# The RWKV-7 recurrence of a two-block kernel: preparation and inversion of each round in one stage

## What is computed

```
S = S * w + (S @ -kk) (kk * a)^T + v k^T
y = S @ r
```

## Time and profile before

| | us |
|---|---|
| median of 3 runs | 2764.68 |
| lowest and highest run | 2762.72, 2766.3 |
| the profiled execution | 2762.08 |
| its span | 2759.1 |
| TensorE, VectorE, ScalarE busy in the span | 2668.9, 1884.4, 1205.4 |

### The profile page before, as it was taken

The page is one execution under the profiler, slowest core; times in us unless marked ns, Lnnn a source line. Parts: engine busy times, 40 slices in busy tenths (PEclk is TensorE's granted clock), DMA queues, the critical chain, the costliest instruction groups (busy, mean ns, idle before and its releaser), DMA issues. The chain is left out here.

```text
span 2759.1 us, 48978 instructions
## 1 busy us (share of the span) xinstructions
PE 2668.9 (97%) x19134; PEld 2281.0 (83%) x19134; DVE 1884.4 (68%) x3427; ACT 1205.4 (44%) x2294; POOL 285.1 (10%) x217
## 2 busy tenths in 40 slices
PE   7988899999999999999999999999999999999998
PEld 5868766778888789998878999989999857899997
DVE  3454668552332588887457888888888767788885
ACT  3232235531212454445256544465444438654444
POOL 2000114422111300001401000010000100100000
PEclk9999889999999999999999999999999999999999
DMA  8250310123232223334303333332333331323331
GB/s 279 63 169 16 111 38 5 62 77 107 92 95 88 77 77 97 110 92 124 92 17 92 89 104 96 104 107 86 109 99 101 83 86 26 92 79 113 92 108 54
DMA packets 369540, 248.89 MB, mean 90 GB/s; under 512 B 28692, under 2 KB 364376, under 8 KB 369312
## 3 DMA queue, kind: packets, MB, share of 16 engines
q1 hardware_dynamic: 368818, 245.18, 30.2%
q10 hardware_dynamic: 494, 0.59, 0.1%
HBM read 241.52 MB, written 2.12 MB: 88 GB/s over the span
## 5 line engine op out<-in xcount | busy, mean ns | idle before, releaser
L3018 ACT CAST dense_wt_hi<-ring 128x512 fp32r<-128x512 f32 x719 | 444.4, 621 | 462.5 <-PE bank L3068 220.5
L3023 DVE TENSOR_TENSOR dense_wt_lo<-ring,dense_wt_hi 128x512 fp32r<-128x512 f32 x719 | 493.6, 689 | 105.8 <-ACT dense_wt_hi L3018 104.4
L3055 PE MATMUL bank<-dense_operand_hi,dense_wt_hi 128*128 128x256 f32 x1248 | 353.7, 283 | 4.2 <-DVE h L3672 4.2
L3057 PE MATMUL bank<-dense_operand_hi,dense_wt_lo 128*128 128x256 f32 x1248 | 353.1, 283 | 0.0
L3056 PE MATMUL bank<-dense_operand_lo,dense_wt_hi 128*128 128x256 f32 x1248 | 353.1, 283 | 0.0
L3068 PE MATMUL bank<-dense_act_hi,dense_wt_hi 128*128 128x512 f32 x832 | 258.4, 392 | 0.8 <-DVE dense_act_lo L3336 0.8
L3068 PE MATMUL bank<-dense_act_lo,dense_wt_hi 128*128 128x512 f32 x832 | 257.1, 390 | 0.0
L3068 PE MATMUL bank<-dense_act_hi,dense_wt_lo 128*128 128x512 f32 x832 | 256.7, 390 | 0.0
L3055 PE MATMUL bank<-feat_hi,dense_wt_hi 128*128 128x256 f32 (+1 forms) x820 | 246.8, 301 | 7.5 <-DVE h L3707 3.2
L3055 PEld LDWEIGHTS bank<-dense_operand_hi,dense_wt_hi 128*128 128x128 f32 x1248 | 238.8, 191 | 12.2 <-issue 5.0
L3057 PE MATMUL bank<-feat_hi,dense_wt_lo 128*128 128x256 f32 (+1 forms) x820 | 245.8, 300 | 0.0
(11 more groups left out here) (726 smaller groups left out, 5429.3 us busy)
## 6 DMA issues: line engine op xcount, KB each, us to landing
ring<-in_ffn_w_up SPq DMA_DIRECT2D x88, 512.0 KB, 3.9
ring<-in_ffn_w_gate SPq DMA_DIRECT2D x88, 512.0 KB, 5.2
ring<-in_ffn_w_down SPq DMA_DIRECT2D x60, 512.0 KB, 4.8
ring<-in_ada_w SPq DMA_DIRECT2D x24, 1024.0 KB, 8.0
ring<-in_ffn_w_down SPq DMA_DIRECT2D x52, 256.0 KB, 3.9
ring<-in_w_ffn_gate SPq DMA_DIRECT2D x11, 1024.0 KB, 5.3
ring<-in_w_ffn_up SPq DMA_DIRECT2D x11, 1024.0 KB, 5.4
ring<-in_w_in SPq DMA_DIRECT2D x8, 1024.0 KB, 6.5
```

What stands on the lines that cost most here:

```text
L3018: self.nc.scalar.copy(self.hi(i), src).then_inc(self.s_high, 1)
L3023: self.nc.vector.tensor_tensor(self.lo(i), self.items[i][1], self.hi(i).bitcast(F32), ALU.subtract).then_inc(self.s_low, 1)
L3055: pe.matmul(out, h[:, w], xh, start=start and k == 0, stop=False, skip_group_check=shared)
L3057: last = pe.matmul(out, l[:, w], xh, start=False, stop=stop and k == 3, skip_group_check=shared)
```

## The change

Preparation and chunk stage of a round become one stage, `rwkv_round_stage`, which both rounds run.
- The lora weights are loaded at the head of `in_proj_stage` into a tile of the mixer, and the Tanh is taken there, ahead of ScalarE's last copy.
- Before the steps, only A and B are made. The decay scan runs on the sigmoid itself (the factor -exp(-0.5) goes into the exponentials' scale), the two difference tiles are gone: the growth shifted by one token is read from the scan's columns, and the end factors are multiplied on. Exponentials: three per group instead of four.
- The value transposes are made before the steps; there are 50 steps.
- VectorE makes RT ahead of step 0's mask and after step 1's, the end factors, key factor and BH after step 5, the scaled keys and K after step 13, KH after step 19. TensorE waits for them by `s_late` in the steps that read them. GpSimd keeps only the diagonal.
- Modulation: chunks 0 to 3 of the round stand between the parts ahead of the steps, chunks 4 to 7 after steps 3, 9, 17 and 19. All eight turns come after the last step, ahead of the state. Two memsets in PSUM take the place of two zero products.
- Filler: four products before the steps; the others are gone.

The diff, cut to its core:

```
+class ModulationSums:
...
+    def clear(self):
+        for b in self.rows:
+            self.nc.vector.memset(self.K.bank[b][:, 0:WC], 0.0).then_inc(self.s_clear, 1)
+    def chunk(self, pe, r):
...
+        for half in range(2):
+            for g in range(4):
+                k = 4 * half + g
+                last = pe.matmul(K.bank[self.rows[r % 2]][32 * g:32 * g + 1, 0:WC], K.coef[:, k:k + 1], w[:, k, :],
+                                 start=half == 0, stop=half == 1)
...
+    def turn(self, pe):
+        K = self.K
+        for r in range(self.count):
+            pe.wait_ge(self.s_row, r + 1)
+            for m in range(2):
+                at = self.first + 2 * (self.at + r) + m
+                last = pe.matmul(K.bank[self.turned][:, at:at + 1], self.row[:, r, m * P:(m + 1) * P], K.k("ones")[:, 0:1], start=True, stop=True)
...
 in in_proj_stage, sync and helper:
+        sp.dma_start(M.wl[0:64, :], io["w_decay_up"][0]).then_inc(K.decay_in, 16)
+        sp.dma_start(M.wl[64:128, :], io["w_aaa_up"][0]).then_inc(K.decay_in, 16)
...
+        if t == len(tiles) - 2:
+            e.wait_ge(box["read"], t)
+            nc.scalar.activation(M.wa[0:64, :], M.wa[0:64, :], ACT.Tanh)
...
-def rwkv_prep_stage(K, M, R, rnd, loads):
-def rwkv_chunk_stage(K, M, R, rnd, y):
+def rwkv_round_stage(K, M, R, rnd, y, loads):
...
+            between = [
+                lambda: put(full(g, w.A, None, 3), [("act", lambda: a.copy(w.at, bank(3)))]),
+                lambda: put(full(g, w.B, w.RT, 3), [("dve", masked(w.rb, 3, "upto"))], 1 + g),
+                lambda: put(full(g, w.BH, None, 3), [("act", lambda: a.copy(w.bht, bank(3)))], 3 + g),
+                None,
+                lambda: put(full(g, w.K, w.A, 3), [("dve", masked(w.akt, 3, "strict"))], 5 + g),
+                lambda: put(full(g, w.KH, None, 3), [("act", lambda: a.copy(w.kht, bank(3)))], 7 + g),
+                lambda: put(full(g, w.K, w.RT, 3), [("dve", masked(w.rk, 3, "upto"))]),
+                lambda: put(full(g, w.akt, w.vt, 3), [("act", lambda: a.copy(w.akt, bank(3)))]),
+            ] + [None] * 2
...
 TensorE:
+                pe.wait_ge(R.wl_in, 32)
 (the four lora products)
+                mod.chunk(pe, 0)
 (norm sums of both groups)
+                mod.chunk(pe, 1)
 (spread of both groups)
+                mod.chunk(pe, 2)
+                pe.wait_ge(s_sig, 4)
                 for e in range(2):
+                    for out, l, r, start, stop in full(e, value(e), None, 1):
+                        last = pe.matmul(out, l, r, start=start, stop=stop)
+                    last.then_inc(s_v, 1)
+                mod.chunk(pe, 3)
+                K.keep_clock(pe, K.bank[0], 4)
+                for n, (g, mms, _, late) in enumerate(steps):
+                    if n < 2:
+                        pe.wait_ge(s_ready, n + 1)
+                    if n == 2:
+                        pe.wait_ge(s_vt, 2)
+                    if late:
+                        pe.wait_ge(s_late, late)
...
+                    if n in (3, 9, 17, 19):
+                        mod.chunk(pe, 4 + (3, 9, 17, 19).index(n))
+                mod.turn(pe)
...
 VectorE:
+                for e in range(2):
+                    dve.wait_ge(s_sig, e + 1)
+                    v.tensor_tensor_scan(W[e].kht, K.k("reset"), W[e].vt, 0.0, ALU.mult, ALU.add).then_inc(s_scan, 1)
+                dve.drain()
+                for e in range(2):
+                    dve.wait_ge(s_sig, 3 + e)
+                    v.scalar_tensor_tensor(W[e].B, W[e].at, -1.0, W[e].bht, ALU.mult, ALU.mult)
+                dve.drain()
+                for e in range(2):
+                    dve.wait_ge(s_exp, 2 * e + 1)
+                    v.tensor_tensor(W[e].A, W[e].at, W[e].T, ALU.mult)
+                    dve.wait_ge(s_exp, 2 * e + 2)
+                    v.tensor_tensor(W[e].B, W[e].B, W[e].rk, ALU.mult).then_inc(s_ready, 1)
+                def receptance(e):
+                    dve.wait_ge(s_grow, e + 1)
+                    v.tensor_tensor(W[e].RT, M.rkv[:, ps[e], :], W[e].kht, ALU.mult).then_inc(s_late, 1)
+                def ends(e):
+                    v.tensor_copy(R.end[:, e, :], chunks(W[e].kht)[:, :, C - 1])
+                    v.tensor_scalar(W[e].akt, W[e].bht, K.p("k_a", ps[e]), oka[:, e:e + 1], ALU.mult, ALU.add)
+                    dve.drain()
+                    v.tensor_tensor(chunks(W[e].BH), chunks(W[e].B), end(e), ALU.mult).then_inc(s_late, 1)
+                def scaled_key(e):
+                    v.tensor_tensor(key(e), key(e), W[e].akt, ALU.mult)
+                    dve.drain()
+                    v.tensor_tensor(W[e].K, key(e), W[e].rk, ALU.mult).then_inc(s_late, 1)
+                def last_key(e):
+                    v.tensor_tensor(chunks(W[e].KH), chunks(W[e].K), end(e), ALU.mult).then_inc(s_late, 1)
+                receptance(0)
...
+                    if n == 1:
+                        receptance(1)
+                    elif n == 5:
+                        for e in range(2):
+                            ends(e)
+                    elif n == 13:
+                        for e in range(2):
+                            scaled_key(e)
+                    elif n == 19:
+                        for e in range(2):
+                            last_key(e)
```

More of the change, by code:

```diff
@@ L2333, in mixer1 @@
         A = Bag()
+        M.wl = sb("wl", [P, 512])
         A.wuq, A.wiq, A.wuk = sb("wuq", [P, 2, 512]), sb("wiq", [P, 2, 512]), sb("wuk", [P, 512])
@@ L2629, in _ @@
                 for e in range(2):
-                    nc.gpsimd.tensor_tensor(chunks(R.W[e].A), wide("eye"), R.end[:, e, :].unsqueeze(2).broadcast_to([P, NCH, C]),
-                                            ALU.mult).then_inc(s_diag, 1)
+                    nc.gpsimd.tensor_tensor(chunks(W[e].A), wide("eye"), end(e), ALU.mult).then_inc(s_diag, 1)
             @block.vector
             def _(dve):
-                for n, (g, _, evacs) in enumerate(steps):
+                mod.clear()
+                for e, p in enumerate(ps):
+                    v.tensor_scalar(W[e].at, key(e), K.p("k_k", p), None, ALU.mult).then_inc(s_kk, 1)
@@ L2656, in _ @@
-                    v.tensor_tensor(y[:, 4 + p, C:T], K.bank[4 * e + 2][:, C:T], yy(R.W[e])[:, C:T], ALU.add)
+                    v.tensor_copy(y[:, 4 + p, 0:C], yy(W[e])[:, 0:C])
+                    v.tensor_tensor(y[:, 4 + p, C:T], K.bank[4 * e + 2][:, C:T], yy(W[e])[:, C:T], ALU.add)
+                mod.vector(dve)
             @block.scalar
             def _(act):
-                for n, (g, _, evacs) in enumerate(steps):
+                a.activation(K.warm[:, :], K.k("eps")[:, 0:1], ACT.Sqrt)
@@ new lines, in _ @@
+                for e in range(2):
+                    act.wait_ge(s_kk, e + 1)
+                    a.activation(W[e].akt, W[e].at, ACT.Square).then_inc(s_sq, 1)
+                mod.row_out(act, 0)
+                for e in range(2):
+                    act.wait_ge(s_norm, e + 1)
+                    a.activation(root[:, e, :], K.bank[4 * e + 3][:, 0:8], ACT.Sqrt).then_inc(s_root, 1)
+                mod.row_out(act, 1)
+                for e, p in enumerate(ps):
+                    act.wait_ge(s_lora, 2 * e + 1)
+                    a.activation(W[e].vt, K.bank[4 * e][:, :], ACT.Sigmoid, bias=K.p("w0", p)).then_inc(s_sig, 1)
@@ new lines, in _ @@
+                for e, p in enumerate(ps):
+                    act.wait_ge(s_lora, 2 * e + 2)
+                    a.activation(W[e].bht, K.bank[4 * e + 1][:, :], ACT.Sigmoid, bias=K.p("a0", p)).then_inc(s_sig, 1)
+                for e in range(2):
+                    act.wait_ge(s_scan, e + 1)
+                    a.activation(chunks(W[e].T)[:, :, 1:C], chunks(W[e].kht)[:, :, 0:C - 1], ACT.Exp, scale=NEG_SQRT_E).then_inc(s_exp, 1)
+                    a.activation(W[e].rk, W[e].kht, ACT.Exp, scale=-NEG_SQRT_E).then_inc(s_exp, 1)
@@ new lines, in _ @@
+                for e in range(2):
+                    act.drain()
+                    a.activation(W[e].kht, W[e].kht, ACT.Exp, scale=NEG_SQRT_E).then_inc(s_grow, 1)
+                for e in range(2):
+                    act.wait_ge(s_v, e + 1)
+                    a.copy(W[e].vt, K.bank[4 * e + 1][:, :]).then_inc(s_vt, 1)
+                for r in (2, 3):
+                    mod.row_out(act, r)
+                if rnd == 0:
+                    a.activation(M.g[:, :], M.g[:, :], ACT.Sigmoid)
+                    a.activation(M.g2[:, :], M.g2[:, :], ACT.Sigmoid)
@@ L2661, in _ @@
+                for n, (g, _, evacs, _) in enumerate(steps):
                     if n_act[n]:
@@ L2679, in rwkv @@
             for rnd in range(2):
-                rwkv_prep_stage(K, M, R, rnd, loads)
-                rwkv_chunk_stage(K, M, R, rnd, y)
+                rwkv_round_stage(K, M, R, rnd, y, loads)
 PAD = 16
```

294 lines of the change are left out of this document (110 added, 184 removed).

## The result

| us | before | after |
|---|---|---|
| median | 2764.95 | 2741.21 |
| lowest and highest run (4 each) | 2762.72, 2766.3 | 2734.51, 2742.93 |
| the profiled execution | 2762.08 | 2734.51 |
| its span | 2759.1 | 2732.7 |

The ratio is 0.992 (95% interval 0.9905 to 0.9935): 23.7 us faster, against 22.3 forecast. The profiled execution is the fastest of its four, 27.6 us under the profiled one of before. It is compared with before by its stretches, and the medians by themselves.

The account below looks back on a forecast made before the run. Four stages run one after the other, 205.1 of 2759.1 us, with no engine the bound all the time. Terms: -15.4 - 15.2 + 2 x 4.15 = -22.3 us, off the median 2764.7: 2742.4, range 2733 to 2753.

Parts of the forecast that it names:

- front: Stage start to the inversion's first product: 13.8 us instead of 29.2 and 29.0, so -15.4 and -15.2 us.
- inversion without turns: Steps of the inversion: value pair gone, -1.95; VectorE's deferred work adds 0.75, 0.55, 0.6 and 1.1 us per round.
- turns: All eight after the last step, 1.2 us hidden: +2.8 us per round, bounds 2.6 and 3.5.
- state and stage end: New modulation columns and coefficients at the stage's end: +0.3 us per round.
- the gap: After step 19: two KH directly ahead of the next pair's masks, +1.1 us; chunk 7 beside them costs nothing.
- the second rival: VectorE bounds the inversion, its bundles count in full, 8.0 us: +5.0 per round, 2752; chance 0.12.
- one fall per round near the first TT: TensorE's clock falls to half there once per round as before, a fall costing 2.5 us; nothing added.
- if more than one such window shows per round: Sign that the prediction is wrong: more than one window of granted clock 0.50 in a round.
- The first, no fall at all: Rival: TensorE's clock falls in neither round, gain 27.3 us, 2737; chance 0.2.
- The third, a fall in the front: Rival: a second fall of TensorE's clock per round, ahead of the inversion: +6 us, 2748; chance 0.13.
- The fourth: Rival: modulation isn't hidden between the steps, four chunks on the path: +4 us per round, 2750; chance 0.05.
- The fifth: Rival: TensorE's clock stays at half through the inversion: +47 us, 2812; chance 0.04.

Follow-up runs that it names:

- first repetition: The changed kernel run again with nothing edited and a new profile: 2739.01 us, ratio 0.9915.
- second repetition: The changed kernel run once more, nothing edited, beside three others: 2740.99 us, ratio 0.9925.
- all moves: Changed kernel with turns in gaps of the inversion, more filler, BH and KH on GpSimd, chunk 7 after step 23: 2733.01 us, ratio 0.9893.
- the bundles: Changed kernel with VectorE making RT, end factors, BH, K and KH of both groups ahead of step 0's mask: 2753.04 us, ratio 0.9973.
- the chunks: Changed kernel with modulation chunks 4 to 7 ahead of the steps, behind chunk 3: 2759.34 us, ratio 0.9987.
- the hats with chunk 7: Changed kernel with BH and KH made by GpSimd inside the inversion and chunk 7 after step 23: 2742.2 us, ratio 0.9921.
- the turns with fillers: Changed kernel with the eight turns spread into gaps between steps and ten more fillers per round: 2731.64 us, ratio 0.9888.
- the hats on GpSimd: Changed kernel with BH and KH made by GpSimd inside the inversion instead of by VectorE: 2741.82 us, ratio 0.9933.

## Why the prediction was right, point by point

By its own steps, in us; the fourth column's fronts and stretches are those of the profiled executions.

| step | forecast, per round | round 0 | round 1 |
|---|---|---|---|
| front | -15.4, -15.2 | -15.05 | -14.88 |
| inversion without turns | +1.05 | -1.93 | -1.51 |
| turns | +2.8 | +3.38 | +2.67 |
| state and stage end | +0.3 | +1.25 | +1.23 |
| sum | -11.25, -11.05 | -12.35 | -12.49 |

(Before, from the first product to the state's: 67.22 and 67.72 us; after: 68.67 and 68.88, with 6.42 and 5.71 from the last step to the state instead of 3.04.)

- **Front.** 14.11 against 13.8, 0.3 too short by the walk. The spread, scans and sigmoids came within 0.3 us of their places; the table loads cost 1.28 and no more. VectorE has A and B of group 0 after 13.45 us, so it is the four fillers that hold the first product to 14.11, as the walk has it. What the walk is set against is less sure: 28.99 is a preparation at a mean clock of 0.83, and at full clock the same one took 26.29. So some 2.7 of round 1's 14.88 come from the execution that was profiled, not from the change. The Trainium skill ("ScalarE: Activation LUTs", section "What ACT_TABLE_LOAD costs") would have a drain of 1.38 us beside each; the trace disagrees, as weighed, and 2748 would have been wrong.
- **Inversion.** By the stretches between turns of T, round 0. First product to first turn: 4.88 before, 5.14 after, so +0.26 where the receptance products were charged 0.75. Then 10.60 and 8.56; without the fall the old one is 8.12, so BH and the factors cost 0.44, charged 0.55. Then 9.25 and 9.95, of which K and its factor are 0.54, charged 0.6. Then 9.33 and 8.45; with KH and chunk 7 both away it is 7.37, so the value pair gave 1.96, charged 1.95, and the gap cost 1.08, charged 1.1. The bundles cost 2.3 in all, not 3.0, and the one term that is clearly off is the first. The gap's reason is only half right: chunk 7, "beside the two KH: nothing", holds it as well. The level that the prediction had not seen, step 4 to step 12, took 11.15 us at full clock, VectorE busy 9.42 of them and TensorE 9.30: of the second rival so much is true that in this level the two are even.
- **The clock.** Here the prediction's place was wrong. It kept one fall per round near the first TT. In the profiled execution there is none there: the inversion without turns comes to -1.93 and -1.51, which is 1.05 less the 2.5 of a fall, -1.45. In its place the clock fell in the turns and the state, which lengthened the state by 1.2 and 0.8 us and round 0's turns by 0.8 (4.46 us, in round 1 at full clock 3.67). In the first repetition it fell at both places in round 1, and in the front of round 1 as well (15.75); by the prediction's own sign, "if more than one such window shows per round", it is wrong there. In the second repetition it fell in the turns and the state alone. That the forecast's total stands is in part luck, since a fall gone and a fall gained nearly cancel. Nor did the change take the fall away: the old inversion ran once in 65.03 us without it. TensorE had the same two waits of 1.51 and 1.22 us there, so these waits alone don't bring the clock down, as the prediction read it. "One fall in each round as now" was read off one execution, and 2.5 us is its price only where it lasts 6.8 us; the one in the repetition's round 1 lasted 3.4 and cost 1.0.
- **The turns** were taken at 2.8 with bounds 2.6 and 3.5; 3.38, of which 0.8 is the low clock, and 2.67. That they were the largest term after the front was right: spreading them gave 5.4 us of median.
- **State and stage end.** The +0.3 for more modulation columns is about right: they cost 0.08 us in round 0 and, with the coefficients, 0.47 in round 1. What the term lacks is the half clock, 1.17 and 0.76.
- **Rivals.** The first, no fall at all, came true in no profiled execution of this kernel; it did in both rounds of the one with all moves. The second is excluded by the bundles: in full they cost over 5 us a round more. The third, a fall in the front, came in round 1 of the first repetition and of five variants, and cost 1.6 us there, not 3. The fourth is excluded by the chunks. The fifth: in the two rounds no stretch at half clock was longer than some 10 us.

Against its own profiled base the forecast is less close: 2739.8, and 2734.51 measured in an execution that is the fastest of its four. The medians differ by 23.7 us here and by 22.7 and 22.5 in the two repetitions.

What stays open is what decides whether the clock falls at the first TT in a given execution. One thing goes with it. Of the nine profiles with the new order (those with chunks or bundles ahead of the steps left out), none has the fall there in round 0. Round 1 has it in the five whose front was lengthened by a fall (15.75 to 15.80 us), and not in the four whose front took 14.11 or 14.12. With fillers in the front and after step 4 none of four rounds had a fall there, but each kernel was profiled once. The two falls in a second level, of the hats with chunk 7 and of the turns with fillers, began within 0.9 us of the end of the two longest stalls of TensorE, 2.23 and 1.96 us; behind stalls of up to 1.71 us none came. The state's small products don't bring the clock down by themselves: behind a full step they ran at 1.00. Whether one-column products alone do wasn't tried. In round 1 of the changed kernel all of them ran at 1.00 (335.33 to 339.00), and the fall began 0.2 us into the state.

## What to carry to other kernels

Ahead of a dependent chain, make only what its first link reads, and put the rest where the chain waits anyway: that was some 12 to 15 us a round here, and cost under 3. Before moving work out of a full gap, look at what else stands in the same gap on the other engines: one of two equal holders removed gives nothing. Products of one column in a row do not go ahead of a stretch that TensorE has to get through, a chain of tiny products for one; spread them between larger ones. A single profiled execution is no base for a term of the clock: look for the same stretch in a second one before pricing it.

## What the runs showed of the hardware

- A busy TensorE is not one at full clock. In 248.78 to 254.28 it reads 99% busy (5.43 of 5.50) at a granted 0.53, nearly the 1.2 GHz level, after 4.46 us of one-column products; behind a full step instead of them, the same products ran at 1.00.
- GpSimd slows some of VectorE's operations that read and write SBUF alone: 0.69 to 1.38 and up to 1.75 for two full inputs, 0.16 to 1.01 for a copy of 8 columns. In the run with the hats on GpSimd, the additions with an input in PSUM (0.69), the transpositions (0.71) and the operation on one tile and columns (L2644, 0.53) stayed as they were beside it. The Trainium skill ("GPSIMD Engine Reference", section "8. Key points") names shared SBUF interfaces, with contention for VectorE instructions with two SBUF inputs or in a two-port mode. The trace agrees for the multiplications; the small copy has one input only, and no run here shows in which mode it ran.
- TensorE can stand still inside a step, with nothing that the profile shows for it: 1.71 us in round 0 of the first repetition, 0 in the first profile, at a granted 1.00 in both.
- Executions of one program differ by 11 us with nothing changed (16 of the changed kernel; 23 of the kernel before in one batch by 13.8), and the mean granted clock (0.983 to 0.988) orders the slowest and the fastest of them. Single profiled executions are to be compared by stage.
